# Folding the merge stage into the expert stage, and packing the query weights by head

## The reference, cut to what matters

```python
# dilated groups mixed by their softmax denominators
wts = softmax(stack(lses, axis=0), axis=0)
od = sum(wts[..., None] * stack(outs, axis=0), axis=0)
br_gla, br_dil, br_mem = og @ w_br_gla, od @ w_br_dil, om @ w_br_mem
gt = sigmoid(gates)                                  # (tokens, 3, 1024)
merged = gt[:, 0] * br_gla + gt[:, 1] * br_dil + gt[:, 2] * br_mem
h = x + merged @ w_out
n2 = rms_norm(h, ln2_g)
# PEER: 8 heads, 2 x 128 keys, top 16 of 16384 experts per head and token
qh = (n2 @ peer_wq).reshape(T, 8, 2, 128)
s = einsum('thcd,hckd->thck', qh, keys)
sv, si = top_k(s, 16)
sc, pos = top_k(sv[:, :, 0, :, None] + sv[:, :, 1, None, :], 16)
gw = softmax(sc)
hpre = einsum('td,thkd->thk', n2, peer_u[eidx])
y = h + einsum('thk,thkd->td', gelu(hpre) * gw, peer_v[eidx])
```

## Time and profile before

| | us |
|---|---|
| median of 3 runs | 4650.23 |
| lowest, highest | 4646.62, 4652.02 |
| the profiled execution, its own time | 4646.97 |
| the profiled execution, its span | 4645.3 |
| busy in the span: PE / DVE / ACT / POOL | 4167.1 / 2470.2 / 1744.6 / 1516.7 |
| last store of merged rows issued | 1922.0 |
| first dot product of the experts | 1980.0 |

### The profile page before, as it was taken

How to read it: one execution, slowest core, us unless ns; L and a number is a source line. 1 busy time by engine, 2 the same in 40 slices (tenths; PEclk the granted TensorE clock), 3 DMA queues, 4 the chain that set the end, 5 groups by cost and what they waited for, 6 DMA issues and landing times.

```text
span 4645.3 us, 55356 instructions
## 1 busy us (share of the span) xinstructions
PE 4167.1 (90%) x18639; PEld 2496.4 (54%) x18639; DVE 2470.2 (53%) x5406; ACT 1744.6 (38%) x4663; POOL 1516.7 (33%) x1389
## 2 busy tenths in 40 slices
PE   7999999998687989899898898998998988988987
PEld 6888888887555764444444344444444444444431
DVE  2111111113843754477667666666676666666665
ACT  2111111113622654244444444444444444444443
POOL 0000000001624531044444444444444444444443
PEclk9999999998788999999999999999999999999999
DMA  8899899794697765599999999999999999999998
GB/s 288 274 323 325 295 319 321 257 300 166 199 349 247 222 184 186 180 424 427 427 427 423 426 421 417 425 422 421 420 419 421 425 417 423 423 416 419 420 418 368
DMA packets 319029, 1635.93 MB, mean 352 GB/s; under 512 B 44721, under 2 KB 87953, under 8 KB 176914
## 3 DMA queue, kind: packets, MB, share of 16 engines
q0 software_dynamic: 162640, 1160.06, 60.0%
q1 hardware_dynamic: 120506, 251.00, 15.9%
q10 hardware_dynamic: 35648, 222.04, 14.2%
HBM read 1547.06 MB, written 311.74 MB: 400 GB/s over the span
## 4 chain that ended last, share of the span: by engine, by line
DMA 30%; PE 18%; ACT 5%; issue 3%; DVE 1%; POOL 0%; DVEq 0%; POOLq 0%; ACTq 0%; PEldq 0%
DMA ex_rows<-scratch_uv,ex_E 30%; PE ex_ps_y L2937 14%; PE ex_ps_q L2885 3%; ACT ex_diag L2636 1%; ACT L2624 1%; ACT L2619 1%; ACT ex_w L2628 1%; ACT ex_gel L2624 1%; PE ex_ps_t L2847 1%; POOL ex_rows L2567 0%; PE ex_ps_y L2931 0%; ACT ex_ex L2619 0%; DVE ex_dots L2781 0%; PE ex_ps_s L2919 0%; DVE ex_rows L2781 0%
## 5 line engine op out<-in xcount | busy, mean ns | idle before, releaser
L2937 PE MATMUL ex_ps_y<-ex_rows,ex_diag 128*128 128x512 f32 (+1 forms) x4224 | 2022.9, 614 | 277.3 <-ACT ex_diag L2636 256.1
L2781 DVE CUSTOM_DVE_ANT_0 ex_rows<-ex_rows,ex_n2u 128x1024 f32<-128x1024 f32 x1056 | 1294.9, 1226 | 868.4 <-DMA ex_rows<-scratch_uv,ex_E 857.8
L2567 POOL DMA_INDIRECT ex_rows<-scratch_uv,ex_E x1056 | 1197.3, 1134 | 1539.3 <-PE ex_ps_y L2937 1395.2
L2937 PEld LDWEIGHTS ex_ps_y<-ex_rows,ex_diag 128*128 128x128 f32 (+1 forms) x4224 | 747.0, 190 | 1401.6 <-ACT ex_diag L2636 711.6
L417 PE MATMUL pj_ps<-pj_w_hi,pj_nT 128*128 128x470 f32 x3072 | 913.3, 377 | 6.2 <-DVE pj_w_lo L253 5.0
L2624 ACT ACTIVATE ex_gel<-ex_dots 128x1 f32<-128x1 f32 x1056 | 214.3, 203 | 1386.6 <-DVE ex_dots L2781 1385.9
L417 PEld LDWEIGHTS pj_ps<-pj_w_hi,pj_nT 128*128 128x128 f32 x3072 | 580.0, 189 | 88.3 <-issue 10.4
L417 PE MATMUL pj_ps<-pj_w_lo,pj_nT 128*128 128x470 f32 x1536 | 577.9, 376 | 0.0
L281 DVE COPY pj_zo<-pj_ps 128x470 f32<-128x470 f32 x96 | 61.4, 646 | 699.8 <-PE pj_ps L417 477.8
L2636 ACT ACTIVATE ex_diag<-ex_ident,ex_w 128x128 f32<-128x128 f32 x1024 | 411.1, 401 | 33.4
L281 ACT COPY pj_zo<-pj_ps 128x470 f32<-128x470 f32 x96 | 51.9, 553 | 804.4 <-PE pj_ps L417 412.5
(11 more groups left out here) (387 smaller groups left out, 3616.7 us busy)
## 6 DMA issues: line engine op xcount, KB each, us to landing
pj_w<-in_w_in POOLq DMA_DIRECT2D x24, 1880.0 KB, 17.7
scratch_z<-pj_zo SPq DMA_DIRECT2D x192, 235.0 KB, 11.1
scratch_uv<-in_peer_u ACTq DMA_DIRECT2D x8, 4096.0 KB, 25.0
scratch_uv<-in_peer_v ACTq DMA_DIRECT2D x8, 4096.0 KB, 42.2
scratch_uv<-in_peer_u ACTq DMA_DIRECT2D x4, 8192.0 KB, 42.0
scratch_uv<-in_peer_v ACTq DMA_DIRECT2D x4, 8192.0 KB, 73.1
out_dk_s<-in_cache_dil_k ACTq DMA_DIRECT2D x8, 4088.0 KB, 42.5
out_dv_s<-in_cache_dil_v ACTq DMA_DIRECT2D x8, 4088.0 KB, 54.7
```

The lines of the kernel that those rows point to most:

```text
L2567: pool.indirect_dma_start(out=rows[:, p % SLOTS, :], out_offset=None, in_=d["uv"], in_offset=bass.IndirectOffsetOnAxis(ap=E[:, turn % 4, k ...
L2781: nc.vector.tensor_tensor_reduce(out=row, in0=row, in1=n2u[:, tile % 2], scale=1.0, scalar=0.0, op0=ALU.mult, op1=ALU.add, accum_out=dots[ ...
L2937: last = nc.tensor.matmul(y[0:n, 512 * c:512 * c + 512], diag[:, p % DIAGS, 0:n], rows[:, p % SLOTS, D + 512 * c:D + 512 * c + 512], start ...
```

## The change

`merge` is emptied, and its work is done inside `experts`. Tiles 0 and 1 are merged before the first turn; tiles 2 to 8 are merged one in each of the turns 0 to 6 (`IN_TURNS`), at fixed places `k`. Merged rows of tiles 0 and 1 stay in SBUF, those of tiles 2 to 8 go through `scratch_h` as before. The softmax over groups is taken for all eight tiles at once at the end of `attend`; the groups are multiplied by DVE and no longer by GpSimd. There is one buffer each for groups, gates, linear-attention rows and turned blocks, where there were two.

SBUF has to hold both: the expert stage has 5 slots for gathered rows until row 120, and 8 from there on (the other three lie in the gate buffer and the turned blocks). The 7 MB of query weights are no longer loaded whole: heads 1 to 7 are streamed through two buffers for the turns 1 to 10 (nine loads of 1 MB), and heads 3 to 7 are loaded once more, to stay, into the branch weights' place once those are used up (`load_held`; heads 5 to 7 after the first tile's output). For these loads, `peer_wq` is moved in `project` by eight transfers of ACT's queue into `scratch_wq`, laid out head by head, so that a head's part for one partition is one run of 8 KB.

```diff
@@ project
+    d["wq_packed"] = nc.dram_tensor("scratch_wq", (PH, P, KD, 256), fp32, kind="Internal").ap()
...
+            for head in range(PH):
+                act.dma_start(d["wq_packed"][head], d["peer_wq"][:, head * 256:(head + 1) * 256].rearrange("(k p) n -> p k n", p=P)).then_inc(wq_moved, 16)
             root(HELD)
             root(HELD + 1)
             last_joins(DEC_B, EARLY)
@@ attend, last part
+                    for g in range(NG):
+                        sp.dma_start(merged.wts[:, :, g, :], d["lse"][g].rearrange("(t p) h -> p t h", p=P)).then_inc(merged.lse_in, 16)
...
@@ merge
 def merge(nc, d):
...
+    pass
@@ experts
+    IN_TURNS = NT - 1
+    FEW, SLOTS = 5, 8
+    ALL_FROM = (IN_TURNS * K + K // 2) // FEW * FEW
+    STREAM = (1, 2, 3, 4, 5, 6, 7, 9, 10)
+    PRODUCT_AT = (5, 6, 8, 9, 10, 11, 13, 14)
...
@@ experts, SP
-            sp.dma_start(wq[:], d["peer_wq"].rearrange("(k p) n -> p k n", p=P)[:, :, 256:]).then_inc(wq_in, 16)
...
+            for b in range(3):
+                load_gate(0, b)
+            load_gla(0)
+            load_x(0)
+            for g in range(2 * PH):
+                sp.dma_start((n2u[:, 1], yo[:])[g // PH][:, (g % PH) * P:(g % PH + 1) * P], d["peer_keys"][g // 2, g % 2]).then_inc(keys_in, 16)
...
+            for turn in range(IN_TURNS):
+                tile = in_turn(turn)
                 if tile + 1 < TILES:
+                    load_groups(tile + 1)
...
+                if turn + 4 < len(STREAM):
+                    load_head(turn + 4)
+                for b in range(3):
+                    if tile + 1 < TILES:
+                        if b == 0:
+                            sp.wait_ge(first, tile + 1)
+                        else:
+                            sp.wait_ge(gated, NPRD * tile + 2 * b)
+                        load_gate(tile + 1, b)
+                sp.wait_ge(added, NPRD * (tile + 1))
+                sp.dma_start(d["h"][tokens(tile), :], a_gla[0:width(tile)]).then_inc(m_stored, 16)
+                if tile + 1 < TILES:
+                    sp.wait_ge(m_stored, 16 * (tile - 1))
+                    load_gla(tile + 1)
+            load_held(3)
+            load_held(4)
@@ experts, GpSimd
-                    if p >= SLOTS:
-                        pool.wait_ge(v_done, p - SLOTS + 1)
+                    if held_before(p) is not None:
+                        pool.wait_ge(v_done, held_before(p) + 1)
+                    elif p >= FEW:
+                        pool.wait_ge(m_stored, 16 * IN_TURNS)
@@ experts, ACT, in row k of a turn
+                    if in_turn(turn) is not None:
+                        if k == 4:
+                            turned_branches(in_turn(turn))
+                        if k == 6:
+                            gate_values(in_turn(turn))
@@ experts, DVE
+            gated_part(1, 0)
+            for part in range(K):
+                route(0, part)
+            gated_part(1, 1)
+            gated_part(1, 2)
+            for part in range(K):
+                route(1, part)
+            gated_part(1, 3)
+            for part in range(3):
+                mixed(2, part)
...
+                    if k == 1 and turn and in_turn(turn - 1) is not None:
+                        gated_part(in_turn(turn - 1), 3)
+                    if tile is not None:
+                        if k == 8:
+                            first_gated(tile)
+                        if k in (9, 12, 14):
+                            gated_part(tile, (9, 12, 14).index(k))
+                        if k in (10, 11, 13) and tile + 1 < TILES:
+                            mixed(tile + 1, (10, 11, 13).index(k))
@@ experts, PE, before the first turn
+            turn_branches(0)
+            product(0, 0)
+            pe.wait_ge(keys_in, 16 * 2 * PH)
+            turn_keys(0)
+            turn_keys(1)
+            product(0, 1)
+            product(0, 2)
+            product(0, 3)
+            turn_merged(0)
...
@@ experts, PE, in row k of a turn
+                    if tile is not None:
+                        if k == 2:
+                            turn_branches(tile)
+                        if k in PRODUCT_AT:
+                            q, half = divmod(PRODUCT_AT.index(k), 2)
+                            product(tile, q, (half,))
```

More of the change, by code:

```diff
@@ L1606, in _ @@
                     act.wait_ge(lsub, 1)
[L1607 removed]
+                    nc.scalar.activation(merged.wts[:], merged.wts[:], ACT.Exp).then_inc(lexp, 1)
         @block.vector
@@ L2547, in _ @@
+            load_held(3)
+            load_held(4)
+            for tile in range(1, TILES):
+                if tile < TILES - 1:
                     load_m(tile + 1)
@@ L2549, in _ @@
                     load_x(tile + 1)
+                if tile == 1:
+                    store_y(0)
+                    for head in (5, 6, PH - 1):
+                        load_held(head)
                 if tile + 1 == NT:
@@ L2803, in normed_rows @@
                                                op0=ALU.mult, op1=ALU.mult).then_inc(n2_done, 1)
+            first_gated(0)
+            for q in range(NPRD):
+                gated_part(0, q)
+            for part in range(3):
+                mixed(1, part)
+            first_gated(1)
             added_rows(0)
@@ L2808, in _ @@
             normed_rows(0)
-            for turn in range(2):
-                for part in range(K):
-                    route(turn, part)
+            gated_part(1, 0)
[6 more added lines that the diff above has]
+            gated_part(1, 3)
+            for part in range(3):
+                mixed(2, part)
             for turn in range(TURNS):
+                tile = in_turn(turn)
                 for k in range(K):
@@ new lines, in product @@
+            def product(tile, q, halves=(0, 1)):
+                n, b, c = width(tile), 1 + q // 2, q % 2
+                if 0 in halves:
+                    pe.wait_ge(aT_out, tile + 1)
+                    if q >= 2:
+                        if tile == 0:
+                            pe.wait_ge(keys_out, 2)
+                        else:
+                            pe.wait_ge(gated, NPRD * tile + q - 1)
+                k0 = BRANCH[b][0]
+                for half in halves:
+                    for k in range(k0 + 2 * half, k0 + 2 * half + 2):
+                        last = nc.tensor.matmul(bank(tile, q)[0:n], aT[:, k, 0:n], wb[:, k, 512 * c:512 * c + 512],
+                                                start=(k == k0), stop=(k == k0 + 3), skip_group_check=True)
+                if 1 in halves:
+                    last.then_inc(prod, 1)
@@ L2943, in sum_row @@
                     pe.sem_inc(y_sum, 1)
-            for turn in range(3):
-                if opens(turn):
-                    turn_rows(turn)
-                queries(turn)
-                scores(turn)
+            pe.wait_ge(d["wb_in"], 32)
+            turn_branches(0)
[7 more added lines that the diff above has]
+            turn_merged(0)
+            for part in range(2 * KD):
+                out_product(0, part)
+            turn_branches(1)
+            product(1, 0)
+            pe.wait_ge(consts_in, 48)
+            turn_rows(0)
+            queries(0)
+            scores(0)
+            product(1, 1)
+            queries(1)
+            product(1, 2)
+            scores(1)
+            queries(2)
+            product(1, 3)
+            scores(2)
             for turn in range(TURNS):
```

532 lines of the change are left out of this document (237 added, 295 removed).

## The result

| | us |
|---|---|
| kernel after, median of 6 runs | 4663.55 (4648.77 to 4668.61) |
| kernel before on the same chip, median of 6 | 4649.12 (4646.62 to 4652.02) |
| ratio | 1.0031, 95% interval 1.0021 to 1.0041 |
| kernel after, profiled execution, own time | 4648.77 |

The change makes the kernel 0.3% slower: 14 us, where 44 were forecast. The profiled execution happens to be the fastest of the six.

A forecast was written before the change was run, and what follows sets the result against it. The prediction took PE to bound projection and merge, and DMA at 425 GB/s the expert turns. 4647 - 99 + 113 + 12 + 18 = 4691 us, 0.9% slower; 8 in 10 from 4632 to 4742.

The forecast's parts named there:

- term 1: Start of the expert stage: the first dot product comes earlier, putting the stream of gathers 99 us ahead.
- term 2: Turns 0 to 6: merge work on PE and DMA makes them longer, +113 us over the 280 before.
- term 3: DMA-bound turns: loading five heads of query weights to stay, 5.24 MB, costs +12 us.
- term 4: Projection, pass 8: the eight moves hold ACT's queue and PE stalls for bank 0, +18 us.
- moves that do not hold ACT: Rival in the projection: term 4 is nothing, total 4673 us; chance 0.10 with the turns as forecast.
- the three owed rows: At the first dot, five rows are loaded instead of eight; three at 2.5 us are owed, lowering term 1's gain.
- These two sums do not overlap perfectly: Turns 0 to 3: DMA's 53.1 us and PE's 51.1 us, split after six rows, make a turn 57.6 us.
- The 2 us a turn for ACT: Turns 0 to 6: ACT's sigmoid and table changes at `k` = 6 cost 2 us each turn, 14 us in all.
- Good overlap: Rival: turns 0 to 6 come down to PE's 345 us, +65 instead of +113, total 4643; chance 0.30.
- The starved case: Rival: five slots starve the gathers in turns 0 to 6, turn 62.7 us, +159, total 4737; chance 0.18.

The follow-up runs named there:

- again: The kernel after, unchanged, run once more: 4657.57 us, ratio 1.0025 to the kernel before.
- moves: The kernel before with only the eight moves of query weights added in the projection, nothing reading them: 4666.01 us, ratio 1.0038.
- spread: The kernel after with one move of query weights at the end of each of passes 0 to 7, instead of one block: 4656.48 us, ratio 1.0017.
- first: The `direct` kernel with tile 0's second merge product made ahead of turning the keys: 4638.99 us, ratio 0.9981.
- direct: The kernel after without the moves, later query weight loads reading `peer_wq` itself in runs of 1 KB: 4644.12 us, ratio 0.9995.
- noswitch: The kernel after with Gelu in place of Sigmoid for the gates from tile 2 on, sparing two table loads a turn: 4659.84 us.
- best: The `first` kernel with eight of the sixteen key loads issued on ACT's queue: 4640.78 us, ratio 0.9988.
- halfprod: The kernel after with half of the merge products' matmuls left out from tile 2 on, all transfers kept: 4647.24 us.
- thin: The kernel after with narrowed gate and group loads from tile 3 on, 1.9 MB less per turn, engine instructions kept: 4657.62 us.
- the seven profiles: Kernel after (two runs, one being `again`), `spread`, `direct`, `noswitch`, `first`, `best`: merged turns as in the kernel after; turns 0 to 6 take 361.4 to 372.3 us.
- few4: The kernel after with four gather slots instead of five until row 120, and seven instead of eight after: 4688.53 us.
- slots5: The kernel before with five slots for gathered rows instead of eight in all 66 turns: 4868.91 us.

## Why the prediction was right in its direction and too high in its size

Terms in us; "measured" is the first profile, with `again` in brackets where it differs:

| step | forecast | measured |
|---|---|---|
| term 1, first row earlier | -99 | -113 |
| term 2, turns 0 to 6 | +113 | +84 (+92) |
| term 3, held heads, turns 7 and 8 | +12 | +15 |
| term 4, the moves | +18 | +15 at the seam; `moves` alone +18 |
| rest | 0 | about 1 |
| sum on 4647 | 4691 | 4649 (4655) |

**Term 4 held.** Mechanism, place (bank 0 in pass 8) and size are those of the forecast; the chance of 0.10 for moves that do not hold ACT was for the wrong side. ACT returned at 786 instead of 791. `spread` adds that moving them elsewhere in the projection does not make them free.

**Term 1 was 14 us too small.** The turning of tile 0's merged rows came 31.0 us after the start of the stage, forecast 30.4. The way from there to the first dot took 55.3 us, not 55.5 + 7.3. About 6 of that come from PE: the same 32 records of the `w_out` product took 14.00 us instead of 16.98, and the queries of head 0 3.84 instead of about 6.6. The granted clock says why: it was 0.82 of full speed from 1927 to 1945 in the kernel before (at its lower level, 0.50, up to 1931, right behind PE's 4 us wait at the stage seam), and 0.98 from 1815 to 1882 in the kernel after. This part of the gain is luck. With the same instructions, the way from the turning to the first dot took 55.2 us in `again` and `first` at 0.99 and 1.00, but 59.8 in `direct`, `noswitch` and `best` at 0.91; 62.8 were forecast. The rest, some 9 us, is the three owed rows (7.5 us), which are nowhere to be seen as a debt of their own (turn 0 took 49.9 us, which term 2 counts), and 2 us of the work of DVE that I had added in full.

**Term 2 is the step that failed**, and in it the sentence "These two sums do not overlap perfectly", with its 25.1 us for the six rows `k` 1 to 6 and so 57.6 us for a turn. (Its base was also 3 us off: the seven turns before took 277.4 us, not 280.) The two sums were right: 21.5 MB at the rate of the trace is 53.1 us, PE's sum 51.1. I let the loads that are released around `k` = 1 to 4 be done while the early rows run. They are not: those rows took 19.5 to 21.7 us, and the other ten 31.2 to 33.7, near the 32.5 forecast. The same 16 DMA engines carry gathers and SP's loads side by side. In turn 2 the groups and the head are issued 13 and 17 us after row 1 and land in the late part, and the DMA engines, to which the forecast gave 28 us of work in the 32.5 of the late part, have a share of 1.00 or more there. `halfprod` shows it by an edit: with every transfer kept and less work for PE, the early rows took 17.1 to 18.1 us.

So turns 1 to 4 took 52.8 to 53.3 us (53.0 to 54.6 in `again`), about the larger of the two sums, which I had only as a lower bound (359; measured 361 and 369). That the larger sum alone sets a turn is not shown. With PE's work down by 7 us a turn, the turns stay at DMA's sum; but with DMA's sum down by 5.5 (`thin`) they stay at 55 instead of PE's 51, and over the seven profiles the turns 1 to 4 take 52.2 to 56.2. Two bounds stand close together: the DMA engines' sum of 53, and PE's work with its waits and at its granted clock, 52.9 to 56.2 us in turns 2 to 4 where the products are whole. Relief on one side wins 12 us or nothing, relief on both 24. How the waits, the clock and the round of the slots share the second bound stays open.

The 2 us a turn for ACT (14 in all) do not show at full load: `noswitch`, which takes away about half of ACT's hold, makes no difference beyond the scatter. The forecast gave the Trainium skill's figure for this ("What ACT_TABLE_LOAD costs" in ScalarE: Activation LUTs), a drain of about 1.38 us beside each load. The chain of turn 2 disagrees: 2005.81 + 1.28 is 2007.09 and the sigmoid starts at 2007.11, and the second load ends where the gelu begins; no gap of that length stands behind a load.

**The rivals.** Good overlap (0.30) had the better mechanism, traffic of early rows that flows in later ones, but it let the turns come down to PE's 345 us and forgot that DMA's own sum is larger; its 4643 is 21 us below the measured 4663.55, and the forecast's 4691 is 27 above. The mean turn was 51.6 to 52.7 us, over its threshold of 50. The starved case is refuted in its size: with fewer slots in flight the landing fell from 14.9 to 9.6 us. Its mechanism is there all the same, one slot further down: `few4` pays 3.8 us a turn, `slots5` 3.3 in the kernel before. By reckoning, five slots leave little to spare in a merged turn: 5 x 53/16 = 16.6 us for a round of some 9.6 + 5. One sign that the forecast gave failed too: turn 8 was to be at 40 us again and took 50.9 (42.9 before); SP issues the last three held heads in it, at 2304.

**Where the gain went.** The 113 us that merging inside the stage wins are paid back by 84 to 92 us in the merged turns, 15 for the held heads in turns 7 and 8, and 15 by the packing moves. The last alone turns a level result into a loss. The kernel scatters between runs: the first six have a median of 4663.55, the ten of `again` 4657.57. The two traces place what varies between them in the merged turns, where PE's granted clock varies as well; whether the clock is the cause stays open.

## What to carry to other kernels

When two stages are laid over each other, add up each engine's work over a turn and take the larger sum as a first estimate from below (53.1 us here, measured 52.9 to 56.2 in turns 2 to 4); a split of the turn by the places where transfers are released overstated the loss here. When the two sums are within a few us, relieving one engine alone brings little. A transfer from HBM to HBM is not free because the DMA engines have room: ask which engine issues it, how long the queue holds it, and what that engine owes next. And count the buffers in flight at the slower pace of the overlapped turn, not at the pace of the stage alone.

## What the runs showed of the hardware

- An issue of eight transfers of 1 MB in runs of 1 KB, HBM to HBM, held ACT for 27.15 us; eight 64 KB loads into SBUF held it for 5.27 us.
- A gather of 1 MB lands in 14.9 us with eight slots in use, 8.3 with five, at DMA rates of 425 and 390 GB/s. The three more slots buy 3.3 us a turn of 40; the eighth buys none (turns with seven take 40 us too).
- PE's granted clock varies from run to run with the same instructions: the product with `w_out` took 14.00 us at 1.00 (1829 to 1843, and again in `again` and `first`), 15.70 in `direct`, 16.99 in `best`, where the clock was 0.50 over its first 5 us, and 16.98 at 0.82 in the kernel before. In the projection of the kernel after, the clock was 0.85 from 780 to 820, behind the 12.8 us stall.
